# Matmuls without a reader put into a two-layer diffusion backbone: three in the first chunk of each output projection, seven in layer 1's route stage

## The chip, the cores and the metric

The kernel runs as one launch on one NeuronCore of a Trainium2 chip. The metric is device time in microseconds (us); lower is better. TensorE is the matmul engine (PE in the profile, PEld its weight loads), ScalarE is ACT, VectorE is DVE, GpSimd is POOL, SyncE is SP and here only issues transfers.

## The reference, cut to what matters

```python
for l in range(DEPTH):                       # 2 layers, D_MODEL 1024, 256 latent + 256 context tokens
    h = modln(x, g_attn[l], sh_a, sc_a)      # context tokens likewise (hc)
    y, yc = token_mixers(h, hc, w_in[l], ...)    # conv + 2 attentions, merged by gates, then m @ w_o
    x = x + gt_a * y
    h2 = modln(x, g_ffn[l], sh_f, sc_f)
    ...
    yt = hier_moe(h2, w_rg[l], b_rg[l], w_re[l], b_re[l], w_g[l], w_u[l], w_d[l])   # 32 experts, top 2
    x = x + gt_f * yt
return rmsnorm(x, g_final)
```

Layer 0 works on all 512 tokens (four tiles of 128), layer 1 after its attention on the 256 latent ones (two tiles). The output projection is `m @ w_o`. The route stage is the norm in front of the experts, the router's logits, the choice of two experts for each token, and the place of each token in its expert's list. Every expert's weights (3 MB in float32) are read from HBM in both layers.

## The kernel before, in words

Each engine runs its own instruction list in a fixed order, and semaphores order them among each other. SP streams all weights through a ring of six buffers of 1 MB; a buffer is loaded again when its reader is done. `mod` chunks (the conditioning matrices) go through the same ring, so TensorE's `mod` matmuls release buffers.

The large products are made in a split form: a weight unit (one eighth of a chunk, 128x256) is rounded by ACT into `w_hi` (L1643), DVE computes the rest `w_lo` (L2044), and TensorE adds three products for each output tile (L1030 in `split_units`, L1211 in `merge`). Four split units can stand ready (AHEAD = 4). In `merge` the branches are gated: DVE multiplies (L2176, counted by `gated`, six for each pair of channel tiles) into the merged tiles, which are rounded (ACT L1722, `merged_hi`) and get a rest (DVE L2157, `merged_lo`). The last two merged tiles, 6 and 7, are finished after merge's last matmul.

`out_proj` makes four chunks of eight units; each unit is 12 matmuls in layer 0 and 6 in layer 1. In ACT's list the end of `gates` and the begin of `out_proj` stand in this order:

```python
merged_hi(5)
for q in range(1, AHEAD):
    split_w(("wo", l, 0), q)      # units 1 to 3 of the first chunk (unit 0 stands ahead of merged_hi(5))
for q in (6, 7):
    merged_hi(q)
...
split_ahead(split_w, ("wo", l, c), ...)   # out_proj: units 4 to 7, then units 0 to 3 of the next chunk
```

DVE has the same order (`merged_lo(6)`, `merged_lo(7)`, then `residual`, which begins with the rests of units 4 to 7). On TensorE `split_units` waits for `w_lo_ready` of each unit, and in the first chunk for `m_lo_ready` of the merged tile too.

After `out_proj` TensorE runs `ffn_columns` (L991, 128 matmuls of two columns), waits for the residual updates, and then in layer 1: `turn_h` (16 transposes of the scaled rows, L980), `route` (router L1240, then the logits turned back, L1246), `mod(1, 5, 0..3)` (L964, 64 matmuls), `ranks` (L1264 to L1269), and `experts`, which begins with `first_x` (16 matmuls L1347 and 16 L1351 that gather the token rows). `turn_h` waits for the rows that DVE (L2021) and ACT scale; ACT (L1588) and DVE (L2032) take the transposes into `hT`; ACT then rounds the token rows (L1758), DVE takes their rest (L2038, `rest_rows`), and only behind that does DVE copy the router's output (L2235) for L1246. `ranks` needs DVE's choice of experts (`pick_ready`), `first_x` needs the selection that DVE computes from the ranks (L2325). SP's ring loads for the first experts (L703) wait for `mod_done` of these four `mod` calls.

`banks` are the eight PSUM banks. The added matmuls multiply the identity (128x128, float32) with 384 columns of the constants.

Of the kernel before, what the change touches and what calls it, by code (L numbers as in the profile page):

```python
# [18 lines left out]
P = 128  # L19
# [188 lines left out]
UNITS = KD // KU  # L208
# [77 lines left out]
def program(nc, t, out):  # L286
    ctx = ExitStack()
    with ctx:
        def sb(name, shape, dt=F32):
            return ctx.enter_context(nc.sbuf_tensor(name, shape, dt))  # L290
# [7 lines left out]
        def sem(name):  # L298
            return ctx.enter_context(nc.semaphore(name))
# [6 lines left out]
        consts = sb("consts", [P, sum(CONST_COLS.values())])  # L306
# [4 lines left out]
        ident = C["ident"]  # L311
# [100 lines left out]
        banks = ctx.enter_context(nc.psum_tensor("banks", [P, 8, 512], F32))  # L412
# [70 lines left out]
        gated = sem("gated")  # L483
# [5 lines left out]
        wo_done = sem("wo_done")  # L489
# [4 lines left out]
        m_lo_ready = sem("m_lo_ready")  # L494
# [456 lines left out]
        def _(pe):  # L951
            mm, turn = nc.tensor.matmul, nc.tensor.transpose

            def mod(l, sec, j2):
                n = MOD_AT[(l, sec)]
                if n == 0 and j2 == 0:
                    pe.wait_ge(cond_ready, 2)
                if n and j2 == 0 and (l, sec) not in ROUTE_BANK:
                    pe.wait_ge(mod_out, n)
                landed(pe, ("mod", l, 4 * sec + j2))  # L960
                w = mod_chunk(("mod", l, 4 * sec + j2))
                for k in (0, 1):
                    for q in range(4):
                        ins = mm(banks[32 * q:32 * q + 32, mod_bank(l, sec), 0:CW], cond32[:, 2 * j2 + k, :],  # L964
                                 w[:, k, q * CW:(q + 1) * CW], start=j2 == 0 and k == 0, stop=j2 == 3 and k == 1)
                ins.then_inc(mod_done, 1)

            def turn_h(l):

                pe.wait_ge(f_col_ready, 2 * (l + 1))  # L970
                for tt in range(QT[l]):
                    pe.wait_ge(f_x_dve, QT0[l] + tt + 1)
                    pe.wait_ge(f_x_act, QT0[l] + tt + 1)
                    s, b = divmod(tt, 2)
                    for k in range(KD):
                        if l == 0 and tt == 2 and k == 6:
                            pe.wait_ge(mod_out, MOD_AT[(0, 5)] + 1)
                        at = (k % 2) * SEQ + b * P
                        rows = htok[:, tt, k * P:(k + 1) * P] if l else htok[:, tt, k::KD]
                        ins = turn(banks[:, k // 2 * 2 + s, at:at + P], rows, ident)  # L980
                        if b and k % 2:
                            ins.then_inc(h_turned, 1)
# [22 lines left out]
            def turn_xn(l, tt, ks):  # L1005

                pe.wait_ge(xn_dve, 4 * l + tt + 1)
                pe.wait_ge(xn_act, 4 * l + tt + 1)
                s, b = divmod(tt, 2)
                if l and b == 0:  # L1010
                    pe.wait_ge(y_gated, tt + 2)
                for k in ks:
                    at = (k % 2) * SEQ + b * P
                    ins = turn(banks[:, k // 2 * 2 + s, at:at + P], xn[tt][:, k::KD], ident)
                    if b and k % 2:
                        ins.then_inc(h_turned, 1)

            def split_units(key, outs, sides, done, rows=None, halfway=None):


                for q in range(UNITS):
                    u = UNIT0[key] + q
                    pe.wait_ge(w_lo_ready, u + 1)
                    if rows is not None:
                        pe.wait_ge(rows[0], rows[1] + q + 1)
                    for out_ap, where in outs:
                        for kk in range(KU):
                            k = q * KU + kk
                            for p_, (a, b) in enumerate(sides(u % AHEAD, kk, k, where)):
                                ins = mm(out_ap, a, b, start=k == 0 and p_ == 0, stop=k == KD - 1 and p_ == 2)  # L1030
                        if q == UNITS - 1:
                            ins.then_inc(done, 1)
                    if q < UNITS - 1:
                        ins.then_inc(unit_done, 1)
                    if halfway and q == UNITS // 2:
                        halfway()

            def chan_sides(ns):
# [178 lines left out]

            def out_proj(l):

                for c in range(4):  # L1220
                    outs = []
                    for tt in range(QT[l]):
                        r = c * QT[l] + tt
                        if r >= 8:
                            pe.wait_ge(upd_ready, 4 * QT0[l] + r - 7)
                        outs.append((banks[:, r % 8, 0:CW], tt))
                    split_units(("wo", l, c), outs, val_sides, wo_done, (m_lo_ready, 8 * l) if c == 0 else None)

            def route(l):

                n = QN[l]
                done = 4 if l == 0 else 8
                for r, k in enumerate(HT_ORDER):
                    if r < 2:
                        pe.wait_ge(hT_act, done + 2)
                        pe.wait_ge(hT_dve, done + 2)
                    else:
                        pe.wait_ge(hT_dve if r % 2 else hT_act, done + r // 2 + 1)
                    p0 = r % 2 * 64
                    ins = mm(banks[p0:p0 + NR, 0, 0:n], w_router[:, k, :], hT[k][:, 0:n], start=r < 2, stop=r >= KD - 2)  # L1240
                ins.then_inc(lgT_done, 1)
                pe.wait_ge(lgT_out, l + 1)
                pe.wait_ge(lgT_out_dve, l + 1)
                for tt in range(QT[l]):
                    for half in range(2):
                        ins = mm(banks[:, 2, tt * NR:(tt + 1) * NR], lgT[half][:, tt * P:(tt + 1) * P], ident[0:NR, 0:NR],  # L1246
                                 start=half == 0, stop=half == 1)
                ins.then_inc(lg_done, 1)

            def turn_rows(tiles):  # L1250

                for tt in tiles:
                    if tt >= 2:
                        pe.wait_ge(th_hi_ready, tt - 1)
                    for k in range(KD):
                        ins = turn(banks[:, ROW_BANKS[tt][k // 4], k % 4 * P:(k % 4 + 1) * P], hT[k][:, tt * P:(tt + 1) * P], ident)
                    ins.then_inc(h_rows, 1)
# [240 lines left out]
            for l in range(DEPTH):  # L1498
                if l == 0:
                    pe.wait_ge(ident_in, 16)  # L1500
                    for j2 in range(4):
                        mod(0, 1, j2)
                        if j2 in (1, 2):
                            for tt in (2 * j2 - 2, 2 * j2 - 1):
                                turn_xn(0, tt, range(KD if tt < 2 else KD - 2))
                    columns(0, 1)
                    pe.wait_ge(col_ready, 1)
                    for j2 in range(4):
                        mod(0, 0, j2)
                    columns(0, 0)  # L1510
                    pe.wait_ge(col_ready, 2)
                    for tt in (2, 3):
                        turn_xn(0, tt, (KD - 2, KD - 1))
                else:
                    pe.wait_ge(col_ready, 4)
                    for tt in range(4):
                        turn_xn(1, tt, range(KD))
                project(l)
                attention(l)
                merge(l)  # L1520
                out_proj(l)

                ffn_columns(l)
                pe.wait_ge(upd_ready, 4 * (QT0[l] + QT[l]))
                if l == 0:
                    for j2 in range(4):
                        mod(0, 5, j2)
                turn_h(l)
                route(l)
                if l == 0:  # L1530
                    turn_rows((0, 1))
                for k, sec in MOD_ROUTE[l][1 - l:2 - l]:
                    for j2 in range(4):
                        mod(k, sec, j2)
                ranks(l)
                if l == 0:
                    turn_rows((2, 3))
                for k, sec in MOD_ROUTE[l][2 - l:]:
                    for j2 in range(4):
                        mod(k, sec, j2)  # L1540
                experts(l)
# [1129 lines left out]
```

## Time and profile before

| | |
|---|---|
| median of 3 runs | 1338.72 us |
| the runs | 1338.72, 1340.43, 1332.54 us |
| the profiled execution, from its first to its last instruction (span) | 1334.4 us |
| mean granted TensorE clock in it | 0.983 |
| PE busy | 1211.1 us, 91% of the span |
| DVE, ACT, POOL busy | 645.5, 440.0, 167.2 us |
| HBM read | 330.53 MB, 269 GB/s over the span |

The profiled execution is a fourth one beside the three runs, and its own time is known only as its span, which lies between the lowest and the median run. "Granted clock" is the share of TensorE's full clock: 1.00 is 2.4 GHz, 0.50 is 1.2 GHz. A name such as "L1030" is a line of the kernel; `x16` counts instructions. A float32 matmul shows as two records.

### The profile page before, as it was taken

How to read it: one execution, taken by the hardware profiler on the slowest of the kernel's cores; microseconds unless marked ns; L12 is line 12 of the kernel's file. 1: busy time of each engine (PE TensorE's matmuls, PEld its weight loads, DVE VectorE, ACT ScalarE, POOL GpSimd, SP SyncE). 2: the span in 40 equal slices, each digit the busy share in tenths (PEclk: the TensorE clock that was granted, in tenths of full speed). 3: DMA queues.
4: the chain of work that ended last, by engine and by line, in shares of the span. 5: the costliest groups of instructions: out<-in, count | busy, mean ns of one | idle time of the engine just before them, and what ended most of it. 6: DMA issues, size and time to landing. Idle time of an engine off the chain costs nothing.

```text
span 1334.4 us, 22176 instructions
## 1 busy us (share of the span) xinstructions
PE 1211.1 (91%) x8966; PEld 926.1 (69%) x8966; DVE 645.5 (48%) x1503; ACT 440.0 (33%) x1049; POOL 167.2 (13%) x208
## 2 busy tenths in 40 slices
PE   5899987999999999899999879999999888889986
PEld 2787854788888967666666449875998865555652
DVE  1544786464345453422222185578767645324334
ACT  3533366533334351000010175356666610000001
POOL 1810000111010210100010221000111100000001
PEclk9899999999999999999999999999999889999998
DMA  9995145423323279999999996338664989999995
GB/s 354 315 354 172 64 140 188 148 95 95 95 95 127 96 266 418 364 404 412 415 378 386 398 253 156 117 123 278 194 187 133 361 327 418 419 416 414 385 374 190
DMA packets 131832, 351.15 MB, mean 263 GB/s; under 512 B 23054, under 2 KB 84726, under 8 KB 108561
## 3 DMA queue, kind: packets, MB, share of 16 engines
q1 hardware_dynamic: 118144, 317.69, 64.4%
q0 software_dynamic: 12304, 30.37, 6.8%
q10 hardware_dynamic: 1280, 1.66, 0.4%
q8 instruction: 73, 1.20, 0.4%
q14 instruction: 31, 0.25, 0.1%
HBM read 330.53 MB, written 28.86 MB: 269 GB/s over the span
## 4 chain that ended last, share of the span: by engine, by line
PE 80%; DVE 8%; DMA 4%; issue 4%; ACT 2%; POOL 1%; SPq 0%; DVEq 0%; ACTq 0%; POOLq 0%
PE banks L1030 34%; PE banks L1288 16%; PE banks L1302 8%; PE banks L1280 6%; PE banks L1211 4%; PE banks L964 3%; PE banks L1136 2%; PE banks L1151 2%; PE banks L1121 1%; DMA expert_rows<-arena,rows_u 1%; DMA ring<-in_w_in 1%; DMA ring<-in_w_mod 1%; DMA ring<-in_w_e_up 1%; DVE w_lo_r L2044 1%; DVE arena L2463 1%
## 5 line engine op out<-in xcount | busy, mean ns | idle before, releaser
L2044 DVE TENSOR_TENSOR w_lo_r<-ring,w_hi_r 128x256 fp32r<-128x256 f32 x480 | 223.0, 475 | 229.5 <-ACT w_hi_r L1643 228.3
L1643 ACT ACTIVATE w_hi_r<-ring 128x256 fp32r<-128x256 f32 x480 | 197.5, 416 | 302.7 <-PE banks L1030 255.3
L1288 PE MATMUL banks<-ring,arena 128*64 128x256 f32 x2016 | 230.9, 381 | 28.1 <-issue 14.1
L1030 PE MATMUL banks<-h_hi_r,w_hi_r 128*128 128x512 f32 (+1 forms) x640 | 221.0, 345 | 6.7 <-DVE h_lo_r L1990 6.5
L1288 PEld LDWEIGHTS banks<-ring,arena 128*64 128x64 f32 x2016 | 162.0, 137 | 86.6 <-issue 36.7
L1030 PE MATMUL banks<-h_lo_r,w_hi_r 128*128 128x512 f32 (+1 forms) x640 | 219.2, 343 | 0.0
L1030 PE MATMUL banks<-h_hi_r,w_lo_r 128*128 128x512 f32 (+1 forms) x640 | 219.1, 342 | 0.0
L1030 PEld LDWEIGHTS banks<-h_hi_r,w_hi_r 128*128 128x128 f32 x640 | 121.7, 190 | 23.7 <-ACT arena L1613 5.0
L1030 PEld LDWEIGHTS banks<-h_lo_r,w_hi_r 128*128 128x128 f32 x640 | 121.8, 190 | 13.8
L1030 PEld LDWEIGHTS banks<-h_hi_r,w_lo_r 128*128 128x128 f32 x640 | 121.6, 190 | 13.9
L1302 PE MATMUL banks<-ring,att 128*64 128x512 f32 x424 | 118.2, 601 | 13.9 <-DVE att L2448 7.4
L1780 ACT ACTIVATE arena<-banks 128x256 f32<-128x256 f32 x32 | 12.3, 384 | 284.7 <-PE banks L1288 284.6
L2441 DVE TENSOR_TENSOR arena<-arena,banks 128x256 f32<-128x256 f32 x32 | 13.5, 421 | 184.5 <-PE banks L1288 178.2
L1030 PE MATMUL banks<-w_hi_r,h_hi_r 128*128 128x256 f32 x320 | 92.9, 290 | 6.4 <-DVE w_lo_r L2044 4.8
L1030 PE MATMUL banks<-w_lo_r,h_hi_r 128*128 128x256 f32 x320 | 91.9, 287 | 0.0
L1030 PE MATMUL banks<-w_hi_r,h_lo_r 128*128 128x256 f32 x320 | 91.8, 287 | 0.0
L1302 PEld LDWEIGHTS banks<-ring,att 128*64 128x64 f32 x424 | 36.6, 137 | 72.5 <-issue 70.1
L1280 PE MATMUL banks<-att_r,h_hi_r 128*128 128x256 f32 x336 | 85.4, 293 | 0.0
L1280 PE MATMUL banks<-att_r,h_lo_r 128*128 128x256 f32 x336 | 81.2, 281 | 0.0
L904 POOL DMA_INDIRECT expert_rows<-arena,rows_u x30 | 29.5, 984 | 396.1 <-ACT arena L1789 167.9
L1280 PEld LDWEIGHTS banks<-att_r,h_hi_r 128*128 128x128 f32 x336 | 63.4, 189 | 16.7 <-issue 16.7
L964 PE MATMUL banks<-ring,cond 128*32 128x256 f32 x768 | 54.8, 419 | 16.7 <-DMA ring<-in_w_mod 15.4
(274 smaller groups left out, 1714.6 us busy)
## 6 DMA issues: line engine op xcount, KB each, us to landing
ring<-in_w_e_gate SPq DMA_DIRECT2D x64, 1024.0 KB, 9.7
ring<-in_w_e_up SPq DMA_DIRECT2D x62, 1024.0 KB, 9.0
ring<-in_w_e_down SPq DMA_DIRECT2D x53, 1024.0 KB, 11.4
ring<-in_w_mod SPq DMA_DIRECT2D x48, 1024.0 KB, 5.8
ring<-in_w_in SPq DMA_DIRECT2D x38, 1024.0 KB, 8.1
expert_rows<-att POOLq DMA_DIRECT2D x23, 512.0 KB, 20.3
ring<-in_w_o SPq DMA_DIRECT2D x8, 1024.0 KB, 5.2
ring<-in_w_branch SPq DMA_DIRECT2D x8, 640.0 KB, 4.6
```

Of the source, the lines that this page charges most:

```text
L904: pool.indirect_dma_start(out=yd, out_offset=bass.IndirectOffsetOnAxis(ap=rows_u[:, p:p + 1], axis=0), in_=y_sb[n % 2], in_offset=None, bo ...
L964: ins = mm(banks[32 * q:32 * q + 32, mod_bank(l, sec), 0:CW], cond32[:, 2 * j2 + k, :], w[:, k, q * CW:(q + 1) * CW], start=j2 == 0 and k ...
L1030: ins = mm(out_ap, a, b, start=k == 0 and p_ == 0, stop=k == KD - 1 and p_ == 2)
L1136: ins = turn(banks[:, 4 + b, q * P:(q + 1) * P], S[s % 3][:, b, q * P:(q + 1) * P], ident)
L1151: ins = mm(banks[HD * e:HD * e + HD, O_BANK, 0:2 * P], vals[:, t0 + q, v0:v0 + HD], PT[e][:, q, :], start=q == 0, stop=q == n - 1)
L1211: ins = mm(outs[half], wt, y, start=k == BRANCH[b][0] and p_ == 0, stop=k == BRANCH[b][-1] and p_ == 2)
L1280: ins = mm(out, h[:, tt, k * P:(k + 1) * P], picked[:, tt, :], start=tt == 0 and h is th_hi, stop=tt == QT[l] - 1 and h is th_lo)
L1288: ins = mm(banks[e * CAP:(e + 1) * CAP, bank, 0:DE], x[:, k, e * CAP:(e + 1) * CAP], w[:, k * DE:(k + 1) * DE], start=k == 0, stop=k == KD ...
L1302: ins = mm(banks[e * CAP:(e + 1) * CAP, Y_BANK + half, :], rows[:, k, e * CAP:(e + 1) * CAP], w[k][:, half * 512:half * 512 + 512], start= ...
L1643: fn(w_hi[:, u % AHEAD, :, :], chunk(key)[:, q * KU:(q + 1) * KU, :], ACT.Copy).then_inc(w_hi_ready, 1)
L2044: v.tensor_tensor(w_lo[:, u % AHEAD, :, :], chunk(key)[:, q * KU:(q + 1) * KU, :], w_hi[:, u % AHEAD, :, :].bitcast(F32), ALU.subtract).th ...
L2441: v.tensor_tensor(hid[n % 2], act_g[n % 2], banks[:, U_BANK, 0:DE], ALU.mult).then_inc(hid_ready, 1)
```

## The change

A helper `keep_awake(bank, n)` issues n matmuls of 384 columns into a PSUM bank; nothing reads what they write. `split_units` gets a parameter for the unit behind which its hook is called. `out_proj` passes a hook for chunk 0 with `pause` 5: TensorE waits until three of the last pair's six gate products are made (bank 4 is then free) and issues three such matmuls. In layer 1's route stage three are issued between the wait for the residual updates and `turn_h`, one between `turn_h` and `route`, and three between `ranks` and `experts`.

```diff
+            def keep_awake(bank, n):
+
+                for _ in range(n):
+                    mm(banks[:, bank, 0:3 * P], ident, consts[:, 0:3 * P], start=True, stop=True)
...
-            def split_units(key, outs, sides, done, rows=None, halfway=None):
+            def split_units(key, outs, sides, done, rows=None, halfway=None, pause=UNITS // 2):
...
-                    if halfway and q == UNITS // 2:
+                    if halfway and q == pause:
                         halfway()
...
             def out_proj(l):
 
+                def filler():
+
+                    pe.wait_ge(gated, 24 * l + 18 + 3)
+                    keep_awake(4, 3)
+
...
-                    split_units(("wo", l, c), outs, val_sides, wo_done, (m_lo_ready, 8 * l) if c == 0 else None)
+                    split_units(("wo", l, c), outs, val_sides, wo_done, (m_lo_ready, 8 * l) if c == 0 else None,
+                                filler if c == 0 else None, 5)
...
                 pe.wait_ge(upd_ready, 4 * (QT0[l] + QT[l]))
+                if l:
+                    keep_awake(2, 3)
...
                 turn_h(l)
+                if l:
+                    keep_awake(1, 1)
                 route(l)
...
                 ranks(l)
-                if l == 0:
+                if l:
+                    keep_awake(5, 3)
+                else:
                     turn_rows((2, 3))
```

## Rows read from the trace of the kernel before

**Rows 1.** The page: busy time of PE, granted clock and DMA share in 40 slices.
```profile
PE 1211.1 (91%) x8966; PEld 926.1 (69%) x8966; DVE 645.5 (48%) x1503; ACT 440.0 (33%) x1049; POOL 167.2 (13%) x208
...
PEclk9899999999999999999999999999999889999998
DMA  9995145423323279999999996338664989999995
```

**Rows 2.** The chain that ended last: start, duration, what.
```profile
128.23 3.88 PE banks L1076 x12
...
425.34 42.07 PE banks L1030 x336
```

**Rows 3.** Timeline of TensorE, first chunk of layer 0's output projection.
```profile
422.80 0.28 PE L1030 MATMUL banks<-w_lo_r,h_hi_r 128*128 128x256 f32 x1
425.34 0.53 PE L1030 MATMUL banks<-w_hi_r,h_hi_r 128*128 128x256 f32 x1 [2.27 <-DVE w_lo_r L2044]
```

**Rows 4.** Timeline of TensorE, first chunk of layer 1's output projection.
```profile
1029.22 0.28 PE L1030 MATMUL banks<-w_hi_r,h_hi_r 128*128 128x256 f32 x1
...
1033.08 0.28 PE L1030 MATMUL banks<-w_lo_r,h_hi_r 128*128 128x256 f32 x1
1035.34 0.39 PE L1030 MATMUL banks<-w_hi_r,h_hi_r 128*128 128x256 f32 x1 [1.97 <-DVE w_lo_r L2044]
```

**Rows 5.** Timeline of DVE, same place: gate products, then rests of four units.
```profile
1028.89 0.74 DVE L2176 TENSOR_TENSOR att<-att,banks 128x256 f32<-128x256 f32 x2
...
1034.86 1.43 DVE L2044 TENSOR_TENSOR w_lo_r<-ring,w_hi_r 128x256 fp32r<-128x256 f32 x4
```

**Rows 6.** Timeline of ACT, same place: merged tile 7, then four units.
```profile
1034.03 0.42 ACT L1722 ACTIVATE h_hi_r<-arena 128x256 fp32r<-128x256 f32 x1 [0.44 <-DVE arena L2216]
1034.36 1.32 ACT L1643 ACTIVATE w_hi_r<-ring 128x256 fp32r<-128x256 f32 x4
```

**Rows 7.** Stretches: length, busy us of PE, PEld, DVE, ACT, POOL, clock, DMA.
```profile
425.34:428.70 3.36, 3.36 (x16) 3.36 (x17) 0.95 (x3) 0.49 (x2) 0.00 (x0) 0.51 0.90 308
...
1036.40:1039.78 3.38, 3.38 (x19) 3.38 (x17) 1.27 (x3) 1.25 (x3) 0.00 (x0) 0.50 1.00 395
...
1061.65:1065.30 3.65, 3.65 (x16) 3.25 (x16) 0.74 (x2) 2.16 (x4) 0.00 (x0) 0.50 1.02 394
...
1070.50:1073.90 3.40, 3.40 (x33) 1.95 (x36) 2.11 (x15) 0.22 (x1) 0.00 (x0) 0.51 0.02 5
...
1077.26:1079.87 2.61, 0.00 (x1) 0.03 (x1) 2.33 (x11) 0.00 (x0) 0.48 (x1) 1.00 0.92 342
...
1080.80:1084.20 3.40, 3.40 (x19) 3.40 (x18) 0.00 (x0) 0.00 (x0) 0.55 (x1) 0.50 1.00 418
```

**Rows 8.** Timeline of TensorE, route stage of layer 1.
```profile
1061.65 3.65 PE L980 MATMUL banks<-consts,arena 128*128 128x128 f32 x16 [2.33 <-DVE arena L2021]
1065.70 2.66 PE L1240 MATMUL banks<-arena,w_router 128*36 128x256 f32 x16 [0.40 <-ACT arena L1588]
1069.99 1.39 PE L1246 MATMUL banks<-consts,att 36*128 36x36 f32 x8 [1.63 <-DVE att L2235]
1071.31 4.94 PE L964 MATMUL banks<-ring,cond 128*32 128x256 f32 x64
```

**Rows 9.** Timeline of TensorE, route stage of layer 0 (granted clock 1.00 there).
```profile
474.47 3.84 PE L980 MATMUL banks<-consts,arena 128*128 128x128 f32 x32
...
496.40 3.66 PE L964 MATMUL banks<-ring,cond 128*32 128x256 f32 x64
```

**Rows 10.** The chain inside layer 1's route stage.
```profile
1065.04 1.01 ACT arena L1588 x2
...
1067.03 2.36 DVE h_lo_r L2038 x2
...
1069.42 0.44 DVE att L2235
```

**Rows 11.** SyncE's issues of the first experts' weights in layer 1 (timeline).
```profile
1073.30 1.62 SPq L703 DMA_DIRECT2D ring<-in_w_e_up  x2
```

## The prediction

> **What bounds the kernel now.** I read the page first [rows 1]: TensorE is busy 91% of the span, so time is won or lost where it stands on the path. The granted clock is full nearly everywhere; the slices with an 8 are the second, the two from 1034 to 1101 us (a slice is 33.4 us), which hold layer 1's output projection and route stage, and the last. The DMA line shows the other limit: in both expert stages the transfers are at 9 tenths or more, so there the stream of expert weights sets the pace once it has begun. Then the chain that ended last [rows 2]: from 425.34 TensorE's L1030 forms one piece of 42.07 us with 336 matmuls, without a wait. Layer 0's output projection has 4 x 8 x 12 = 384 of them, so the chain picks it up behind the first 48, which is four units. That count matters below.
>
> Then TensorE's timeline around the two first chunks [rows 3, 4], with DVE's and ACT's lists beside it [rows 5, 6], the stretches with their granted clock [rows 7], and for the route stage TensorE's timeline, the chain and SyncE's issues [rows 8, 10, 11]. The reader is to see three idle places of 2.27, 1.97 and 2.33 us in front of the out-projection's remainder (layers 0 and 1) and of `turn_h`, and one of 2.61 us behind `ranks` [rows 3, 4, 7, 8], and that at or soon after each of them the clock is at 0.50 or 0.51 for the next stretch of 3.4 us or longer, while TensorE works.
>
> **The price of an added matmul.** The nearest row is L1076, also float32, 128x128 by 384 columns: 12 records, two for each of six matmuls, in 3.88 us [rows 2], 0.647 us each at full clock. Three cost 1.94 us, seven 4.53 us; at half clock twice that. The whole change adds 13 matmuls, 8.4 us of TensorE at full clock.
>
> **Output projections.** Where does the hook stand against the idle place? Layer 1: from 1029.22 to 1033.08 there are 24 matmuls in 0.12 us steps (first and last in [rows 4]), six for each unit, so units 0 to 3 are done when TensorE stops. The idle time ends with DVE's `w_lo` [rows 4]. ACT and DVE show why: four splits in a row, 1034.36 to 1035.7 and 1034.86 to 1036.3 [rows 6, 5], which in both lists are units 4 to 7 and stand behind merged tiles 6 and 7. So TensorE waits in front of unit 4. Layer 0 is the same: 48 matmuls before, 336 behind [rows 2, 3]. The hook stands behind unit 5. There units 6 and 7 are split already (DVE's four end at 1036.3, and TensorE leaves unit 5 at 1036.9 or so, 12 matmuls behind 1035.34), tile 7's rest is made before them, and the gate product it waits for is over by 1029.3, the third of its pair [rows 5]. Nothing waits there, so nothing hides the matmuls: they stand between two units of a TensorE-bound stretch, and units, residual updates, norm and, through the `mod` matmuls, the release of the ring follow later by their length. The added wait itself costs nothing.
>
> The idle place stays empty, and so does its effect on the clock: in layer 0 the clock is at 0.51 from 425.34 on, in layer 1 at 0.50 from 1036.40 on, for 3.4 us each [rows 7]. What they cost, 3.4 / 2 = 1.7 us each, isn't given back. The added matmuls run partly in such a stretch in layer 1 and then take longer themselves, but the real ones that they displace run at full clock instead, so the sum is 1.94 us again. Bounds: 0, if something behind takes up the delay (no wait in the 42.07 us piece says so), and 3.88 us at half clock throughout. I take the row: +1.94 and +1.94, **+3.9 us**.
>
> **Route stage, in front of `turn_h`.** These three do stand in an idle place: TensorE is free for 2.33 us until 1061.65 [rows 8], so they hide if they run at full clock (1.94 us). Before, all 16 transposes ran at 0.50 [rows 7]: 3.65 us, 0.228 us each, against 3.84 / 32 = 0.12 us in layer 0 [rows 9]. The router, ACT and DVE take over in pieces, so not all of it counts: the first pair that ACT can take is complete after ten transposes, 10 x 0.108 = 1.1 us sooner; from there ACT's four L1588, about 0.48 us each [rows 10], set the pace. Router time isn't on the path: it ends at 1068.36, while its output is copied only at 1069.42, behind the 2.36 us of L2038 [rows 8, 10]. So keeping the clock is worth at most 1.1 us. If the clock falls while they run, they end late: at worst 3.88 against 2.33, +1.55 us. That ground is real: in front of the three lie 128 matmuls of two columns (ending 2.33 us before 1061.65), so the whole lull before `turn_h` is only half filled. I take -0.5 us, nearer to the gain because at least the second half of the lull is now dense work.
>
> A sentence of the Trainium skill speaks against the change here. The row shows half clock through all 16 transposes [rows 7], but also full clock in layer 0's 32 [rows 9]. The page "TensorE: Matmul & The Clock Gate", section "Part 4: PE-mode transpose", says that transposes do not count as TensorE activity as matmuls do. By that rule the clock would be lost again during `turn_h` whatever stands in front, and the -0.5 of this part would be 0; layer 0's row, where it stayed full, speaks against it.
>
> **In front of `route`.** One matmul, 0.65 us at full clock, 1.29 at half, against 0.40 us of idle time [rows 8]. The router has 1069.42 - 1068.36 = 1.1 us of slack, so it costs nothing at full clock and at most 0.2 us late at half. 0.
>
> **`mod`.** No matmul is added between `route` and `mod`, and the idle 1.63 us before L1246 stay. The 64 matmuls took 4.94 us, against 3.66 in layer 0 at full clock [rows 8, 9]; the first 2.6 us of them ran in the slow stretch that ends at 1073.9 [rows 7]. How much of the 1.3 us comes back depends on when the clock turns against the program. Bounds -1.3 and +0.5, I take -0.5: the stage begins a little sooner and is denser in front.
>
> **Behind `ranks`.** TensorE is idle for 2.61 us with full clock and then runs `first_x`, 3.4 us of it at 0.50 [rows 7]. Three matmuls fit in with 0.67 us to spare, and the clock should stay: -1.7 us on TensorE. Is that on the path? SyncE got the release of the first weights at 1073.30, through `mod` [rows 11]; in the stretch before, the DMA share was 0.02, afterwards 0.92 to 1.00 [rows 7] and then 9 tenths for the rest of the stage [rows 1]. When the stream begins is settled before `ranks`. A faster `first_x` lets TensorE reach the weights sooner and wait for them. So from 0 to -1.7, I take -0.1. At half clock they would cost 3.88 - 2.61 = +1.3 on TensorE.
>
> **Sum.** +1.94 + 1.94 - 0.5 + 0 - 0.5 - 0.1 = **+2.8 us** against the profiled execution: 1334.4 becomes 1337.2. That execution lies below the median of the three runs, 1338.72; the four known executions have a mean of 1336.5. I add the 2.8 to 1337.6, midway between that mean and the median: **1340.4 us**. The four spread over 7.9 us, more than any term here; a difference within 1%, 13 us, is what a measurement of this kernel can't tell from none with certainty, and I forecast such a one.
>
> **Rivals.**
>
> *The change does what its words say* (0.18): everything added hides and the clock stays up. Output projections: nothing added, 1.7 us back each; route stage: -1.1, -1.3 and up to -1.7. With all of it 3.4 + 4.1 = 7.5 us less, 1330; if only the route stage behaves so and the projections cost their 3.9, it is -0.2, 1337.5. For it: TensorE's waits are real and the clock rows fit. Against it: the count of units before the idle time.
>
> *The lull fillers come too late* (0.2), slower. Its place is in front of `turn_h` and behind `ranks`; it decides once the clock has fallen before or while they run, above 2.33 us and 2.61 us for three. Then +1.55 and +1.3, some 0.2 in front of `route`, and 3.9 from the projections: +6.9, 1344.5. For it: the tiny matmuls didn't hold the clock before. Against it: it was still full from 1077.26 to 1079.87 [rows 7].
>
> *Gaps of this size don't cost the clock* (0.07): then the fillers save nothing and only the 3.9 remain, 1341.5. The same page, section "Why this matters for your kernels", warns only of idle gaps longer than any of these. The rows speak against that here: after 2.27 us of idle time the clock was 0.51 [rows 3, 7].
>
> *My forecast*, projections +3.9 and the route stage -2.5 to 0 (0.55): 1339 to 1341.5.
>
> **From these to the numbers.** No case reaches 13 us in either direction; the largest are -7.5 and +6.9. Faster by over 1%: 0.01; slower by over 1%: 0.02, both for what I haven't seen; within 1%: 0.97. The range takes in my forecast, the late fillers and the partial form of the first rival, with a few us for where the median falls among executions that differ by 7.9 us: 1333.5 to 1346. Left out is the full gain of 7.5 us.
>
> **What would show it.** In the changed trace, records of 384 columns should stand between units 5 and 6, 72 (layer 0) and 36 (layer 1) L1030 matmuls into the chunk, with the idle 2 us still in front of unit 4 and no idle time before the records; and each first chunk should be longer by 1.9 us. The stretch behind the idle time should still be at half clock. In front of `turn_h` idle time should be near zero, the transposes faster than 0.228 us on average, and behind `ranks` `first_x` at 1.00 with the first L1302 waiting for its weights. Wrong would be the prediction if L1030's idle place were behind unit 5 in the new trace, if the stretches after it ran at full clock, or if the end of layer 1's expert stage moved with `first_x` instead of with `mod`.

## The result, and the profile after

| | kernel before | changed kernel |
|---|---|---|
| median | 1339.38 us (20 runs) | 1343.87 us (20 runs) |
| ratio, 95% interval | | 1.0040 [1.0026, 1.0054] |
| the same in us | | +5.4 [3.5, 7.2] |
| span of the profiled execution | 1334.4 us | 1336.1 us |
| mean granted clock of that execution | 0.983 | 0.987 |

The change makes the kernel slightly slower. It was forecast at 1340.4 us and within 1%; the sum of its terms was +2.8 us. The profiled execution of the changed kernel is the fastest of its 20 runs (1337.9 us), and none has a higher clock; over all 20 the mean granted clock is 0.981. The kernel before had 0.978 on average over 87 runs, those with which the experiments below are compared. Intervals in us are here always those of the ratio, times 1339.3. Lines have moved: L1030 is L1035 now, L980 is L985, L1240 L1251, L1246 L1257, L1264 L1275, L1347 L1358, L1288 L1299, L2044 L2061 (L2055 where the route stage's matmuls are left out). The added matmuls are L971.

The page of the changed kernel, busy time, granted clock and DMA share in 40 slices [beside rows 1]:
```profile
PE 1216.3 (91%) x8992; PEld 928.9 (70%) x8992; DVE 645.2 (48%) x1503; ACT 439.9 (33%) x1049; POOL 166.9 (12%) x208
...
PEclk9899999999999999999999999999999999999998
DMA  9995145423323279999999995338664989999995
```
There are 26 more records on TensorE, two for each of 13 matmuls. The two slices with an 8 at layer 1's output projection and route stage are gone: less of them ran at half clock. Time didn't follow it.

TensorE's timeline of the changed kernel [beside rows 3, 4, 8]: start, us, what, idle time before it and what ended it.
```profile
425.88 0.39 PE L1035 MATMUL banks<-w_hi_r,h_hi_r 128*128 128x256 f32 x1 [2.26 <-DVE w_lo_r L2061]
...
430.35 2.10 PE L971 MATMUL banks<-consts 128*128 128x384 f32 x6
...
1036.47 0.39 PE L1035 MATMUL banks<-w_hi_r,h_hi_r 128*128 128x256 f32 x1 [1.99 <-DVE w_lo_r L2061]
...
1038.49 3.25 PE L971 MATMUL banks<-consts 128*128 128x384 f32 x6
...
1062.46 2.20 PE L971 MATMUL banks<-consts 128*128 128x384 f32 x6
1064.88 2.19 PE L985 MATMUL banks<-consts,arena 128*128 128x128 f32 x16 [0.22 <-DVE arena L2038]
1066.90 0.81 PE L971 MATMUL banks<-consts 128*128 128x384 f32 x2
1067.88 2.01 PE L1251 MATMUL banks<-arena,w_router 128*36 128x256 f32 x16 [0.17 <-DVE arena L2049]
1072.38 1.05 PE L1257 MATMUL banks<-consts,att 36*128 36x36 f32 x8 [2.48 <-DVE att L2252]
1073.36 3.66 PE L964 MATMUL banks<-ring,cond 128*32 128x256 f32 x64
1077.56 0.43 PE L1275 MATMUL banks<-att,consts 128*128 128x64 f32 x2 [0.55 <-DVE att L2290]
...
1078.47 2.18 PE L971 MATMUL banks<-consts 128*128 128x384 f32 x6
1081.68 2.14 PE L1358 MATMUL banks<-att_r,h_hi_r 128*128 128x256 f32 x16 [1.02 <-DVE att_r L2342]
```
The idle 2.26 and 1.99 us of the projections stand where they stood. The added records come after them, with no idle time in front: the engine is handed work while work is waiting. In the route stage it is the other way round. Of 2.33 us in front of `turn_h` 0.22 are left, and the transposes take 2.19 us for 3.65.

The same stretches by granted clock [beside rows 7] (the eighth number of a line, behind the five engines):
```profile
426.34:429.70 3.36, 3.36 (x19) 3.36 (x18) 0.91 (x3) 0.42 (x1) 0.00 (x0) 0.51 0.90 293
430.30:432.30 2.00, 2.00 (x9) 1.20 (x9) 0.43 (x1) 0.42 (x1) 0.00 (x0) 1.00 0.52 205
1037.40:1040.80 3.40, 3.40 (x11) 2.43 (x10) 0.88 (x3) 0.83 (x2) 0.00 (x0) 0.50 1.01 401
1064.88:1067.00 2.12, 2.06 (x17) 1.85 (x18) 0.27 (x1) 1.47 (x3) 0.00 (x0) 1.00 0.95 336
1073.36:1077.02 3.66, 3.65 (x65) 1.97 (x64) 3.07 (x22) 0.22 (x1) 0.00 (x0) 1.00 0.42 116
1081.68:1085.72 4.04, 4.03 (x32) 3.83 (x32) 1.21 (x4) 0.68 (x2) 0.55 (x1) 1.00 1.01 424
```
Both projections still have their half-clock stretch. In layer 0 the added matmuls ran after it, at full clock; in layer 1 mostly in it. In the route stage the clock was 1.00 throughout, where the transposes had 0.50 for all of their time, and `mod` and `first_x` for more than half of it.

### The profile page after: what moved, and what is told of

Same layout as the page of the kernel before. It is cut to its first block, busy times and chain, and to the rows that moved or that the text cites. A ratio compares the mean times of both kernels' runs of the same rounds, so it can differ in the third digit from the quotient of the medians.

```text
span 1336.1 us, 22227 instructions
## 1 busy us (share of the span) xinstructions
PE 1216.3 (91%) x8992; PEld 928.9 (70%) x8992; DVE 645.2 (48%) x1503; ACT 439.9 (33%) x1049; POOL 166.9 (12%) x208
## 4 chain that ended last, share of the span: by engine, by line
PE 80%; DVE 9%; issue 4%; DMA 3%; ACT 2%; POOL 1%; SPq 0%; DVEq 0%; ACTq 0%; POOLq 0%
PE banks L1035 34%; PE banks L1299 16%; PE banks L1313 8%; PE banks L1291 6%; PE banks L1216 4%; PE banks L964 2%; PE banks L1141 2%; PE banks L1156 2%; PE banks L1126 1%; DMA expert_rows<-arena,rows_u 1%; DMA ring<-in_w_in 1%; DMA ring<-in_w_mod 1%; DVE w_lo_r L2061 1%; DVE arena L2480 1%; DVE att L2147 1%
## 5 line engine op out<-in xcount | busy, mean ns | idle before, releaser
L2061 DVE TENSOR_TENSOR w_lo_r<-ring,w_hi_r 128x256 fp32r<-128x256 f32 x480 | 222.8, 474 | 234.1 <-ACT w_hi_r L1660 232.8
L1299 PE MATMUL banks<-ring,arena 128*64 128x256 f32 x2016 | 231.2, 381 | 27.4 <-issue 13.3
L1035 PE MATMUL banks<-h_hi_r,w_hi_r 128*128 128x512 f32 (+1 forms) x640 | 221.9, 347 | 5.6 <-DVE h_lo_r L2007 5.5
L1299 PEld LDWEIGHTS banks<-ring,arena 128*64 128x64 f32 x2016 | 161.8, 137 | 86.4 <-issue 36.4
L1035 PE MATMUL banks<-h_lo_r,w_hi_r 128*128 128x512 f32 (+1 forms) x640 | 220.0, 344 | 0.0
L1035 PE MATMUL banks<-h_hi_r,w_lo_r 128*128 128x512 f32 (+1 forms) x640 | 219.8, 343 | 0.0
L1035 PEld LDWEIGHTS banks<-h_hi_r,w_hi_r 128*128 128x128 f32 x640 | 122.4, 191 | 22.5 <-ACT arena L1630 5.0
L1035 PEld LDWEIGHTS banks<-h_hi_r,w_lo_r 128*128 128x128 f32 x640 | 122.3, 191 | 14.0
L1035 PEld LDWEIGHTS banks<-h_lo_r,w_hi_r 128*128 128x128 f32 x640 | 122.5, 191 | 13.8
L1313 PE MATMUL banks<-ring,att 128*64 128x512 f32 x424 | 118.2, 601 | 14.4 <-DVE att L2465 7.3
L1035 PE MATMUL banks<-w_hi_r,h_hi_r 128*128 128x256 f32 x320 | 92.9, 290 | 6.4 <-DVE w_lo_r L2061 4.8
L1035 PE MATMUL banks<-w_hi_r,h_lo_r 128*128 128x256 f32 x320 | 91.5, 286 | 0.0
L1035 PE MATMUL banks<-w_lo_r,h_hi_r 128*128 128x256 f32 x320 | 91.4, 286 | 0.0
L1313 PEld LDWEIGHTS banks<-ring,att 128*64 128x64 f32 x424 | 36.7, 137 | 73.4 <-issue 71.1
L1035 PEld LDWEIGHTS banks<-w_hi_r,h_hi_r 128*128 128x128 f32 x320 | 62.1, 194 | 10.1 <-DVE w_lo_r L2061 5.6
## 6 DMA issues: line engine op xcount, KB each, us to landing
ring<-in_w_e_down SPq DMA_DIRECT2D x53, 1024.0 KB, 10.8
```

Source lines behind the costliest of these rows:

```text
L1299: ins = mm(banks[e * CAP:(e + 1) * CAP, bank, 0:DE], x[:, k, e * CAP:(e + 1) * CAP], w[:, k * DE:(k + 1) * DE], start=k == 0, stop=k == KD ...
L1313: ins = mm(banks[e * CAP:(e + 1) * CAP, Y_BANK + half, :], rows[:, k, e * CAP:(e + 1) * CAP], w[k][:, half * 512:half * 512 + 512], start= ...
L2061: v.tensor_tensor(w_lo[:, u % AHEAD, :, :], chunk(key)[:, q * KU:(q + 1) * KU, :], w_hi[:, u % AHEAD, :, :].bitcast(F32), ALU.subtract).th ...
```

## The experiments

Each timed kernel was compared with the kernel before on the same chip. Labels: "proj" is the output projections' part, "route" layer 1's route stage. To read pieces of a run that are shorter than its scatter, I took some instructions that every profile has as landmarks, and the time from one's start to the next's: the first matmul of an output projection, the first of `ffn_columns`, SyncE's first issue of layer 1's expert weights, TensorE's first matmul on them (L1299), the matmul near the end that ends an idle time of 3.65 us ("last wait"), and the end of the span. All in us, from the timelines:

| profile | projection, layer 0 | projection, layer 1 | layer 0's `ffn_columns` to layer 1's projection | layer 1's `ffn_columns` to first issue | to L1299 | to last wait | to the end |
|---|---|---|---|---|---|---|---|
| before | 50.18 | 27.94 | 561.88 | 16.14 | 29.82 | 244.21 | 277.27 |
| changed | 52.10 | 30.01 | 560.56 | 14.12 | 26.94 | 242.63 | 275.69 |
| whole_again | 52.08 | 30.07 | 570.15 | 14.14 | 26.94 | 243.77 | 276.77 |
| proj_only | 52.10 | 29.89 | 564.93 | 15.83 | 29.80 | 244.51 | 277.56 |
| proj_x4 | 57.88 | 34.18 | 563.11 | 14.36 | 29.13 | 244.08 | 277.15 |
| layer0_x4 | 56.40 | 27.95 | 569.03 | 14.93 | 29.73 | 244.69 | 277.77 |
| layer1_x4 | 50.16 | 35.84 | 562.24 | 14.93 | 29.22 | 244.39 | 277.45 |
| route_only | 50.10 | 27.92 | 562.87 | 15.58 | 29.18 | 244.77 | 277.63 |
| rank_only | 50.17 | 27.94 | 563.00 | 14.38 | 27.11 | 242.41 | 276.45 |
| unit3_only | 48.67 | 26.45 | 568.13 | 15.83 | 29.82 | 245.04 | 278.11 |
| unit3_route | 48.66 | 26.47 | 563.25 | 14.12 | 26.86 | 243.39 | 276.44 |
| unit3_route_fill | 48.67 | 26.45 | 565.70 | 14.11 | 26.86 | 243.91 | 276.98 |
| early_only | 48.66 | 27.96 | 563.25 | 12.00 | 29.67 | 243.94 | 277.00 |
| mod_early | 48.66 | 26.46 | 561.49 | 10.65 | 27.27 | 241.78 | 274.84 |

**The projections' matmuls alone.** The whole change without the three `if l: keep_awake(...)` of the route stage.

> Only the output projections' matmuls (three behind unit 5 of each first chunk) are left of the change. My theory: nothing hides them, so the whole run is 3.9 us slower than the kernel before; in the trace the idle time of 2.0 to 2.3 us is still in front of unit 4, no idle time is in front of the records of 384 columns, and the stretch after the idle time is at half clock in both layers. Rival, the change does what its words say: 0 to 3.4 us faster, no half-clock stretch. If the whole change's 5.4 us come from here, there is something beyond their own length.

Measured: 1343.87 against 1339.26 us, ratio 1.0034 [1.0020, 1.0048], +4.6 us [2.7, 6.4]; the forecast 3.9 lies inside. In the profile both idle places are in front of unit 4, and the projections are 1.92 and 1.95 us longer. For the projections the rival that the change does what its words say is out. The largest part of the loss is here.

**Their price, four times over.**

```diff
-                    keep_awake(4, 3)
+                    keep_awake(4, 12)
```

> Only the output projections' matmuls, twelve behind unit 5 in place of three: 24 in all at 0.647 us each. If each costs exactly its own length on the path, 15.5 us over the kernel before, 11.6 over proj_only; each layer's piece from unit 4 to ffn_columns is 7.8 us longer. If some of proj_only's 4.6 us was something else (a side effect of adding any at all), the slope is under 11.6; if the delay is taken up by the weight stream, much less.

Measured: 1352.8 us, ratio 1.0104 [1.0067, 1.0141], +13.9 us [9.0, 18.9] for 24 matmuls (still without those of the route stage), against 15.5. Then each layer alone, the hook passed for one `l` only:

> Twelve matmuls behind unit 5, in layer 0's first output-projection chunk alone. My theory: 7.8 us on TensorE's path up to ffn_columns. proj_x4's profile had its route stage 3.1 us shorter than before, so some of it is taken up there by weights that have landed meanwhile: +4.7 to +7.8 us at the end. If the surplus of the whole change over its sum sits in layer 0's expert stage, whose length differed by 9 us between profiles, this is above 7.8.

> The same twelve in layer 1 alone. My theory: nothing takes the delay up, since the weight stream of the last expert stage begins with mod: +7.8 us at the end, and layer 0 unchanged. The two together should give proj_x4's 13.9 us. If the surplus sits behind layer 1, above 8.

Measured: 1.0056 [1.0035, 1.0076], +7.5 us [4.7, 10.2] for layer 0, and 1.0062 [1.0043, 1.0081], +8.3 us [5.8, 10.8] for layer 1; twelve matmuls are 7.8. That is 0.647 us each at the end of the program, within intervals of 2 to 3 us either way. In the table twelve make a projection 7.7 to 7.9 us longer, counted from 50.2 or 27.9 where the clock fell at unit 4 and from 48.7 or 26.4 where it didn't. Whether layer 0's route stage takes up a part of its twelve can't be told at this interval. The profiles hint at it: from `ffn_columns` to the first expert's matmul layer 0 took 38.3 us in proj_x4 and 38.7 in layer0_x4, and 40.0 to 43.1 in the twelve others, with three behind unit 5 41.4 to 41.5, as in the kernel before. So three weren't taken up there, and of twelve some 2 to 3 us may have been.

**At the idle place instead.** The hook's unit, without the route stage's matmuls:

```diff
-                                filler if c == 0 else None, 5)
+                                filler if c == 0 else None, 3)
```

> As proj_only, but the three matmuls stand behind unit 3, where the trace shows the idle time. My theory: they hide (1.94 us in 2.14 to 2.4 us) and the clock stays full, so unit 4 starts when it did and the 3.4 us behind it lose no 1.7 us: 3.4 us faster than the kernel before over both layers, if what follows passes it on, 7.3 us faster than proj_only. Rival, gaps of this size don't cost the clock or a filler doesn't hold it: 0. If the three end later than the split of unit 4: up to 1 us slower in each layer.

Measured: 1338.77 us, 0.9985 [0.9969, 1.0001], -2.0 us [-4.2, +0.1]: between theory and rival by time, 6.6 us better than proj_only by the difference of the two. The profiles decide on the mechanism. TensorE's timeline of unit3_route, layer 1:
```profile
1032.88 2.10 PE L971 MATMUL banks<-consts 128*128 128x384 f32 x6
1035.02 0.39 PE L1035 MATMUL banks<-w_hi_r,h_hi_r 128*128 128x256 f32 x1
```
and its stretches (length, busy time of five engines, clock, DMA):
```profile
1032.88:1034.98 2.10, 2.10 (x8) 0.95 (x6) 1.85 (x6) 1.66 (x6) 0.00 (x0) 1.00 1.03 339
1034.98:1038.98 4.00, 3.96 (x33) 3.97 (x34) 2.60 (x7) 2.11 (x7) 0.00 (x0) 1.00 1.03 410
```
Three fit: unit 4 follows 2.14 us after the first, as late as before, and runs at 1.00. In the four kernels with this hook both projections took 48.66 or 48.67 and 26.45 to 26.47 us, eight times out of eight 1.5 us less than before. Of the 20 projections with an empty idle place (the matmuls behind unit 5 taken off) three were that short as well, layer 0's in early_only and layer0_x4 and layer 1's in proj_x4, and no half clock stands at their unit 4: the same 2.0 to 2.3 us of idle time cost the clock in 17 of 20. So a filled place is worth 1.3 us on average, not the 1.7 of my expectation.

**The route stage alone.** The whole change with `None` for the hook.

> Only the seven matmuls of layer 1's route stage are left. My theory: -1.1 us against the kernel before (bounds -2.5 and 0), nearly all from transposes and mod at full clock; the gain of first_x on TensorE, up to 1.7 us, does not reach the end, because the weight stream begins with mod. Rival, the fillers come too late: +1 to +3 us, with turn_h or first_x starting later than their inputs. The measured 5.4 us of the whole change against 3.9 from the projections would need +1.5 here.

Measured: 1337.22 us, 0.9984 [0.9971, 0.9998], -2.1 us [-3.9, -0.3]. Not late: `turn_h` starts 4.49 us behind `ffn_columns`' start, as before. But the profile shows what stays open to the clock. TensorE's timeline of route_only:
```profile
1062.32 2.19 PE L985 MATMUL banks<-consts,arena 128*128 128x128 f32 x16 [0.20 <-DVE arena L2038]
...
1069.82 1.66 PE L1257 MATMUL banks<-consts,att 36*128 36x36 f32 x8 [2.48 <-DVE att L2252]
1071.41 6.35 PE L964 MATMUL banks<-ring,cond 128*32 128x256 f32 x64
```
The idle place of 2.48 us in front of L1257, which the change leaves empty and makes longer than the 1.63 of before, was followed by half clock this time, and `mod` needed 6.35 us for the changed kernel's 3.66. The same 2.5 us kept the clock in both profiles of the changed kernel and in unit3_route: one of four.

**Behind `ranks` alone.** Only `keep_awake(5, 3)` is left.

> Only the three matmuls behind ranks in layer 1. My theory: first_x runs at full clock and the first expert's matmuls start 1.7 us sooner after ranks, but the expert stage behind is as much longer, since the weight stream began with mod: 0 us at the end (0 to -0.5). Rival, TensorE sets the expert stage's pace: -1.7 us at the end.

Measured: 1336.98 us, 0.9983 [0.9966, 0.9999], -2.3 us [-4.6, -0.1]. My 0 is just outside the interval; the -0.5 to which my range reached and the rival's -1.7 are inside it. In the table its first issue is at 14.38, L1299 at 27.11 and the last wait at 242.41, 1.8 us less than before. At the end of the span 0.8 us of it are left: around the last wait half clock lasted 6.8 us in this profile and 3.4 us in every other. Nor do the 1.8 us come from `first_x` alone: the first issue was sooner too (14.38 for 16.14), because `mod` ran at full clock in this profile (3.66 us for 4.94), and no added matmul stands in front of it.

**All in their idle places.** The whole change with 3 for 5:

> The whole change, with the output projections' matmuls behind unit 3 instead of unit 5. My theory: the sum of unit3_only and route_only, -3.4 and -1.1, 4.5 us faster than the kernel before and some 8 to 10 us faster than the whole change. Rival, a gain in the projections is lost again in the route stage because the clock falls there instead: less than the sum, near 0.

Measured: 1334.62 us, 0.9980 [0.9958, 1.0003], -2.7 us [-5.6, +0.4]; its median lies 9.3 us under the changed kernel's, and by the ratios it is 8.1 us better. The idle place in front of `mod` filled too:

```diff
                 ins.then_inc(lgT_done, 1)
+                if l:
+                    keep_awake(1, 3)
                 pe.wait_ge(lgT_out, l + 1)
```

> unit3_route with three more matmuls between the router and the turned logits (L1246), where TensorE is idle for 2.5 us in front of mod. In two profiles so far (route_only, unit3_only) mod ran at half clock and took 5.3 to 6.4 us, in two at full clock and took 3.7. My theory: with the lull filled mod always takes 3.7 us, the release of the first weights comes 1 to 2 us sooner in such executions, and the median is 0.5 to 1.5 us under unit3_route, some 4 to 6 under the kernel before. Rival, the clock isn't what delays the release: no difference from unit3_route.

Measured: 1337.17 us, 0.9984 [0.9964, 1.0003], -2.1 us [-4.8, +0.4]. No gain over unit3_route can be told, and its profile is the same up to L1299 (26.86), since unit3_route had full clock there anyway. Whether the filler there pays stays open.

**Work instead of filler, and the stream's begin.** In the kernel before, two of the four `mod` calls moved into the router's shadow:

```diff
                 ins.then_inc(lgT_done, 1)
+                if l:
+                    for j2 in range(2):
+                        mod(1, 5, j2)
                 pe.wait_ge(lgT_out, l + 1)
...
                 for k, sec in MOD_ROUTE[l][1 - l:2 - l]:
-                    for j2 in range(4):
+                    for j2 in range(2 if l else 0, 4):
```

> The kernel before with no added matmul: in layer 1 the first two of the four mod calls stand between the router and the turned logits, where TensorE was idle for 1.63 us. They take 1.8 us at full clock and 3.6 at half. My theory: the weight stream of layer 1's experts begins with mod, so its release comes 2 to 3 us sooner and the end about 2 us; the turned logits and the ranks come up to 2 us later at half clock, which the stream covers. Rival, the chain through ranks and first_x sets the end: 0, or up to 1.5 us slower.

Measured: 1338.76 us, 1.0001 [0.9983, 1.0018], no difference. The release did come sooner, 12.00 us behind `ffn_columns` for 16.14; the last wait only 0.3 us sooner. By time alone my 2 us aren't excluded (the interval reaches down to -2.3); by the profile the theory that the stream's begin alone sets the end fell. SyncE's issues in early_only, and the DMA share (last but one in a line) behind them:
```profile
1068.46 1.19 SPq L703 DMA_DIRECT2D ring<-in_w_e_up  x2
1071.40 1.19 SPq L703 DMA_DIRECT2D ring<-in_w_e_gate  x2
1081.08 0.33 SPq L727 DMA_DIRECT2D consts<-in_w_e_down  x1
...
1089.83 1.35 SPq L703 DMA_DIRECT2D ring<-in_w_e_up  x2
```
```profile
1074.46:1078.46 4.00, 1.08 (x8) 0.97 (x8) 3.58 (x17) 0.20 (x1) 0.63 (x1) 0.71 1.01 424
1078.46:1082.46 4.00, 3.87 (x18) 3.90 (x19) 0.73 (x2) 0.00 (x0) 0.55 (x1) 0.50 0.46 184
```
and the same place of the kernel before:
```profile
1079.30:1083.30 4.00, 3.43 (x19) 3.46 (x20) 1.17 (x3) 0.00 (x0) 0.40 (x1) 0.69 0.99 396
1083.30:1087.00 3.70, 2.14 (x17) 1.97 (x15) 2.15 (x6) 1.93 (x4) 0.15 (x1) 0.88 0.97 365
```
Four chunks are issued sooner, land sooner, and then the queue runs dry (0.46): SyncE's next issues, the spare weights of L727, wait for the gate rows to be written out, and the ring loads behind them (1089.83) for the first expert's matmuls. Those come with L1299, whose start hasn't moved (29.67 for 29.82). So the stream has two gates, the release by `mod` and the first expert's matmuls; here the first alone was opened, and next to nothing came of it.

**Both gates.** unit3_route with the same two calls moved:

> unit3_route and early_only together: three matmuls behind unit 3 of the first output-projection chunks, seven in layer 1's route stage as in the change, and two mod calls in the router's shadow. My theory: the gains add, 4 us under the kernel before from the clock (unit3_route measured 2.7 by the ratio and 4.6 by the medians) and 2 from the earlier release, so 4 to 6 us. Rival, the clock keepers and the earlier mod serve the same release: no more than unit3_route.

Measured: 1335.08 us, 0.9974 [0.9960, 0.9989], -3.5 us [-5.4, -1.5]. Of all versions its interval lies farthest below 1, and it has the lowest last wait (241.78). That it beats unit3_route isn't shown by time: the medians are 1335.08 and 1334.62.

The other half of the two gates shows in front of the first L1313 (L1302 before). TensorE's timeline of the changed kernel, second group of L1299, and the same group of the kernel before:
```profile
1096.46 3.67 PE L1299 MATMUL banks<-ring,arena 128*64 128x256 f32 x32
1101.19 3.67 PE L1299 MATMUL banks<-ring,arena 128*64 128x256 f32 x32 [1.06 <-issue]
```
```profile
1096.12 7.13 PE L1288 MATMUL banks<-ring,arena 128*64 128x256 f32 x64
```
The changed kernel begins this group 36.09 us behind `ffn_columns` for 38.96, 2.9 us sooner, and then stands idle in the middle of it. From the first L1299 to the first L1313 its idle time is 1.7 us for 0.7, and the gain is down to 1.6 us there, which is what the last wait has. In the five profiles with L1299 at 26.9 to 27.1 and the release at 14.1 to 14.4 this idle time is 1.2 to 2.0 us; in mod_early, with L1299 at 27.3 and the release at 10.65, it is 0.7. That fits the two gates: each holds back what the other has gained. It isn't proven: the profile names no releaser for this idle time, so that it is a wait for weights is my reading, and route_only, with both late (15.58 and 29.18), has 1.5 us of it as well.

**The changed kernel again.**

> The changed kernel once more, unaltered, because its parts measured +4.6 (projections) and -2.1 us (route stage), 2.5 together, and the whole 5.4. If the parts add up, this gives +2 to +4 us; if they hurt each other, above 5. In the trace the piece from unit 4 to ffn_columns should be 1.9 to 2.1 us longer than before in both layers, the piece from ffn_columns to the first expert's matmuls 0.6 to 2.9 us shorter, the expert stage behind it longer by 1 us or more.

Measured: 1343.01 us, 1.0024 [1.0002, 1.0046], +3.2 us [0.3, 6.2]. The profile's pieces are those of the first one in both projections and from `ffn_columns` to L1299, although its span is 1346.4 us: from layer 0's `ffn_columns` to layer 1's projection it took 570.15 us, where the first had 560.56. That piece, 560.6 to 570.2 us over all profiles without order by kernel, holds layer 0's experts and the gathering of their rows, and is most of the scatter between the profiles.

## Why the prediction was right, and where not

**Direction and size class**: right. Within 1%, slower by a few us, because the projections' matmuls stand behind unit 5 and the idle place in front of unit 4. The 1340.4 was the +2.8 on a base of 1337.6, which 20 runs put at 1339.4. So of the 3.5 us between it and the median of 1343.9 the base made 1.8 (one of the four numbers in it was a span, and a span is 1.8 us shorter than the time of its run: 1336.1 and 1337.9 in the changed kernel), and the change 1.7 by the medians, 2.6 by the ratio. That a difference below 13 us can't be told from none with certainty was wrong: 20 runs on each side put this one at 3.5 to 7.2.

**Output projections, +3.9 us**: right. +1.92 and +2.07 us in the changed kernel's profile, +4.6 [2.7, 6.4] as a kernel of its own, 7.5 and 8.3 us for twelve matmuls in either layer. That the displaced half clock doesn't alter the sum was right too: in layer 1 they took 3.25 us, mostly in the slow stretch, and the projection grew by 2.1. (The 24 matmuls in front of the idle place don't stand in even steps of 0.12 us, as I wrote: two short waits lie among them, and they take 3.86 us from first to last start. Their count, on which the place rests, is right.) The price of 0.647 us from L1076 holds: six records in 1.94 us on the chain of the changed kernel, with 24 and 312 L1035 around them, the 336 of before:
```profile
425.88 4.63 PE banks L1035 x24
430.51 1.94 PE banks L971 x6
432.44 37.42 PE banks L1035 x312
```

**In front of `turn_h`, -0.5 us**: they fit, as the row of 2.33 us said. With full clock the turned logits (L1257) start 12.01 us behind `ffn_columns` for 12.83, 0.8 us sooner, between my -0.5 and the bound of -1.1. The clock held from `ffn_columns` to the router in all six profiles of kernels with them; in all eight without them it fell, 2.3 to 5.6 us behind `ffn_columns`' start. The rule that transposes don't count as activity as matmuls do (the Trainium skill, "TensorE: Matmul & The Clock Gate", "Part 4: PE-mode transpose") didn't change the time here: all 16 ran at 1.00, and the clock didn't fall right behind them.

**In front of `route`, 0**: right; the router still ends before its output is wanted.

**`mod`, -0.5 us**: the size depends on the execution, as forecast: 3.66 us in the changed kernel, 6.35 in route_only. What I hadn't seen is that a sooner router ends in a longer wait in front of L1257 (2.48 us for 1.63), so the change makes the lull in front of `mod` longer.

**Behind `ranks`, -0.1 us**: this step failed. When the stream begins is settled before `ranks`, as I wrote, but the end doesn't depend on that alone. Five profiles with L1299 at 26.9 to 27.1 and the release at 14.1 to 14.4 have their last wait at 243.2 on average, three with 29.1 to 29.7 and 14.4 to 14.9 at 244.4: 1.2 us for 2.4 us on L1299, half passed on. The release differs too between the two groups, by 0.6 us, but early_only shows that alone passing on only 0.3 of 4.1. The sign that I had named, the first L1302 waiting for its weights, came one group earlier: 1.06 us of idle time within the second group of L1299.

**The sum.** The route stage as a whole, ffn_columns to last wait: 243.6 on average in the four profiles that have exactly its seven matmuls, 244.5 in the six that have none and no moved `mod`. That is -0.9 us, near the -1.1 that I had put together from partly wrong terms. The pieces give +3.1 us for the changed kernel; measured were +5.4 [3.5, 7.2] and +3.2 [0.3, 6.2]. The first interval excludes 3.1 by a little, the second doesn't. Whether something of up to 2 us is left, and where, stays open: the projections' part (+4.6) and the route part (-2.1) give 2.5 with intervals that are too wide to say that they don't add, and the piece in the middle scatters by 9.6 us between profiles.

**The rivals.** "Does what its words say" is out for the projections and true in the main for the route stage, where only a part of the gain reached the end. "Lull fillers come too late" was not seen in the changed kernel: none of them delayed what follows. It can happen: in mod_early the three behind `ranks` met half clock and took 3.54 us, and `first_x` came 0.2 us later than in unit3_route, with no idle time left in front. "Gaps of this size don't cost the clock" is out as a rule, though 3 of 20 did not: the idle places of 2.0 to 2.3 us in front of unit 4 were followed by half clock in 17 of 20, and by full clock in 8 of 8 when filled.

## What to carry to other kernels

Before you put filler into an idle place, count the instructions between the last landmark and the idle time and find the one that waits; two units beside it, the same three matmuls cost their whole length instead of bringing 1.3 us back. A filler must also be shorter than the wait at full clock, and it is worth only what reaches the next gate: follow the gain to whatever paces the stage behind, and check that all gates of a weight stream move, not the first alone. The mean clock rose, from 0.983 to 0.987 in the profiles and from 0.978 to 0.981 over many runs, while the kernel got slower, so judge such a change by the pieces between fixed instructions.

## What the runs showed of the hardware

The same idle place of 2.0 to 2.3 us, in the same program order, was followed by 3.4 us at half clock in 17 of 20 cases and by full clock in three. One profile of the kernel before can therefore not tell what filling a place is worth; it takes several, or a variant that is always filled. In front of `turn_h` it was plainer: behind `ffn_columns` and 2.3 us of idle time the clock fell in eight of eight profiles, and with three matmuls of 1.94 us in the idle time in none of six.
